# Exchanging the halves of queries and keys: four shifted ScalarE copies, or transfers inside SBUF begun by GpSimd

## The reference, cut to what matters

```python
def apply_rope(t, cos, sin):
    t32 = t.astype(jnp.float32)
    t1, t2 = t32[..., :HEAD_DIM // 2], t32[..., HEAD_DIM // 2:]
    return jnp.concatenate([t1 * cos - t2 * sin, t2 * cos + t1 * sin], axis=-1).astype(t.dtype)

def hybrid_mixer(h, cos, sin, w_in, ...):
    proj = h @ w_in
    q, k, v, x_lru, gate = jnp.split(proj, [...], axis=-1)
    q = apply_rope(q.reshape(bsz, seq, N_Q_HEADS, HEAD_DIM), cos, sin)
    k = apply_rope(k.reshape(bsz, seq, N_KV_HEADS, HEAD_DIM), cos, sin)
    ...
```

## Time and profile before

| | |
|---|---|
| runs, median (range) | 1223.01 us (1222.08 to 1223.96), 3 runs |
| profiled execution, own time | 1217.96 us |
| its span, first to last instruction | 1216.1 us |
| granted TensorE clock, mean | 0.975 of 2.4 GHz |
| PE busy | 1165.7 us, 96% |
| VectorE busy | 864.0 us, 71% |
| ScalarE busy | 545.4 us, 45% |
| GpSimd busy | 13.1 us, 1% |
| HBM traffic | 127 GB/s over the span |

### The profile page before, as it was taken

How to read it: one execution, slowest core, us unless ns; L and a number is a source line. 1 busy time by engine, 2 the same in 40 slices (tenths; PEclk the granted TensorE clock), 3 DMA queues, 4 the chain that set the end, 5 groups by cost and what they waited for, 6 DMA issues and landing times.

```text
span 1216.1 us, 16091 instructions
## 1 busy us (share of the span) xinstructions
PE 1165.7 (96%) x6588; PEld 1010.2 (83%) x6588; DVE 864.0 (71%) x1337; ACT 545.4 (45%) x775; POOL 13.1 (1%) x35
## 2 busy tenths in 40 slices
PE   7989888999899999999999999999999999999995
PEld 7977688988788888888999778988888888888895
DVE  8899988778876777777586997478753656346645
ACT  5579634454324431444346894435531444134430
POOL 4000000000000000000000000000000000000000
PEclk8999988999999999999999999989999999999998
DMA  9632547044684448643222221303333323333212
GB/s 359 232 103 71 190 142 240 1 156 164 219 281 166 150 139 268 222 156 111 83 68 89 69 70 53 105 1 123 103 95 96 104 87 104 91 100 103 88 53 70
DMA packets 44937, 155.78 MB, mean 128 GB/s; under 512 B 5056, under 2 KB 7360, under 8 KB 44864
## 3 DMA queue, kind: packets, MB, share of 16 engines
q1 hardware_dynamic: 44720, 154.23, 38.2%
q10 hardware_dynamic: 144, 0.52, 0.1%
HBM read 152.64 MB, written 2.10 MB: 127 GB/s over the span
## 4 chain that ended last, share of the span: by engine, by line
PE 78%; DVE 12%; DMA 4%; ACT 3%; issue 2%; SPq 1%; DVEq 0%
PE ps L1833 77%; DMA sb_stage<-in_ada 2%; DVE sb_wL L1089 2%; DMA sb_raw<-in_w 2%; DVE sb_R L1559 1%; DVE sb_y L1148 1%; ACT sb_R L778 1%; DVE sb_adaw L1095 1%; DVE sb_x L1152 1%; DVE sb_y L1170 1%; DVE sb_y L1358 1%; ACT sb_hH L605 0%; DVE sb_mL L1380 0%; DVE sb_ssqv L1318 0%; DMA sb_vw<-in_ada 0%
## 5 line engine op out<-in xcount | busy, mean ns | idle before, releaser
L1833 PE MATMUL ps<-sb_hH,sb_wH 128*128 128x512 f32 (+1 forms) x1184 | 424.7, 364 | 7.7 <-ACT sb_hH L605 5.2
L1833 PE MATMUL ps<-sb_hH,sb_wL 128*128 128x512 f32 (+1 forms) x1184 | 418.2, 359 | 0.0
L1833 PE MATMUL ps<-sb_hL,sb_wH 128*128 128x512 f32 (+1 forms) x1184 | 395.1, 358 | 2.7 <-DVE sb_hL L1177 2.7
L1833 PEld LDWEIGHTS ps<-sb_hH,sb_wH 128*128 128x128 f32 x1184 | 228.8, 193 | 43.5 <-ACT sb_hH L605 6.0
L1833 PEld LDWEIGHTS ps<-sb_hH,sb_wL 128*128 128x128 f32 x1184 | 228.7, 193 | 31.7
L1833 PEld LDWEIGHTS ps<-sb_hL,sb_wH 128*128 128x128 f32 x1184 | 214.0, 192 | 35.5 <-DVE sb_hL L1177 3.3
L558 ACT ACTIVATE sb_wH<-sb_raw 128x1024 fp32r<-128x1024 f32 x174 | 181.5, 1050 | 138.3 <-DMA sb_raw<-in_w 138.1
L1089 DVE TENSOR_TENSOR sb_wL<-sb_raw,sb_wH 128x1024 fp32r<-128x1024 f32 x174 | 211.4, 1219 | 38.3 <-ACT sb_wH L558 38.1
L1833 PE MATMUL ps<-sb_mH,sb_wH 128*128 128x256 f32 (+1 forms) x608 | 207.0, 341 | 3.7 <-ACT sb_mH L992 3.5
L1833 PE MATMUL ps<-sb_mL,sb_wH 128*128 128x256 f32 (+1 forms) x608 | 205.9, 339 | 1.7 <-DVE sb_mL L1533 1.7
L1833 PE MATMUL ps<-sb_mH,sb_wL 128*128 128x256 f32 (+1 forms) x608 | 205.3, 338 | 0.0
(11 more groups left out here) (223 smaller groups left out, 1098.3 us busy)
## 6 DMA issues: line engine op xcount, KB each, us to landing
sb_raw<-in_w SPq DMA_DIRECT2D x174, 512.0 KB, 3.7
sb_adaw<-in_ada SPq DMA_DIRECT2D x48, 512.0 KB, 4.4
sb_stage<-in_ada SPq DMA_DIRECT2D x24, 512.0 KB, 11.2
sb_vw<-in_ada SPq DMA_DIRECT2D x24, 512.0 KB, 4.6
sb_side<-in_w SPq DMA_DIRECT2D x8, 512.0 KB, 4.9
sb_raw<-in_w SPq DMA_DIRECT2D x8, 384.0 KB, 14.6
sb_x<-in_x SPq DMA_DIRECT2D x4, 512.0 KB, 5.3
out<-sb_x SPq DMA_DIRECT2D x4, 512.0 KB, 2.9
```

Of the source, the lines that this page charges most:

```text
L1833: return nc.tensor.matmul(out, a, b, start=start, stop=stop, **kw)
```

## The change

ScalarE no longer writes the four shifted blocks. It makes one plain copy of the pair's columns, all 128 partitions, from PSUM to one of two new buffers `rraw`. GpSimd, whose program gets twelve such steps at its end, waits for that copy (`raw_copied`) and begins four transfers, each of 32 partitions by 2 KB (1 KB for narrow pairs), from the copy to the neighbour's block of `swaps`. Each adds 16 to the semaphore of its buffer, so VectorE waits for 64 more on it per turn. The scratch columns of `rsx` move onto columns of `gain1` to make room.

```diff
-        tiny = sb("tiny", [P, 132])
+        tiny = sb("tiny", [P, 128])
...
-        sdx, rsx = tiny[:, 124:128], tiny[:, 128:132]
+        sdx, rsx = tiny[:, 124:128], tiny[:, 96:100]
         edge = sb("edge", [P, GRP, BACK])
+        rraw = [sb("rraw0", [P, SEQ])[:, :], sb("rraw1", [P, SEQ])[:, :]]
...
-        swap_ready, v_pad = sem("swap_ready"), sem("v_pad")
+        raw_copied, swap_ready, v_pad = sem("raw_copied"), [sem("swap_even"), sem("swap_odd")], sem("v_pad")
...
             GTS(nspl[:, :, :], s3, -16.0, 0.0, ALU.mult, ALU.add).then_inc(sp_ready, 1)
+
+            def rope_swaps(l, h, i):
+
+                r = rope_no(l, h, i)
+                cols = slice(0, (2 if i < 2 else 1) * HALF)
+                pool.wait_ge(raw_copied, r)
+                for q4 in range(4):
+                    o = q4 ^ 1
+                    nc.gpsimd.dma_start(swaps[r % 2][32 * q4:32 * q4 + 32, cols],
+                                        rraw[r % 2][32 * o:32 * o + 32, cols]).then_inc(swap_ready[r % 2], 16)
+
+            for l in range(DEPTH):
+                for h in range(2):
+                    for i in range(GRP // 2):
+                        rope_swaps(l, h, i)
...
-                for q4 in range(4):
-                    o = q4 ^ 1
-                    last = nc.scalar.activation(swaps[rope_no(l, h, i) % 2][32 * q4:32 * q4 + 32, cols],
-                                                pair_bank(h, i)[32 * o:32 * o + 32, cols], ACT.Copy)
-                last.then_inc(swap_ready, 1)
+                nc.scalar.activation(rraw[rope_no(l, h, i) % 2][:, cols], pair_bank(h, i)[:, cols],
+                                     ACT.Copy).then_inc(raw_copied, 1)
...
-                dve.wait_ge(swap_ready, r)
+                dve.wait_ge(swap_ready[r % 2], 64 * ((r + 1) // 2))
```

## The result

The changed kernel took 1233.24 us (1232.90 to 1234.33, 4 runs), the kernel before 1222.61 us (1222.08 to 1223.96, 4 runs): ratio 1.0094 (95% interval 1.0082 to 1.0107), so slower by 10.6 us between the medians and 11.5 by the ratio. The profiled execution took 1232.90 us.

A forecast was written before the change was run, and what follows sets the result against it. It took TensorE, busy 96% of the span, as the bound, with ScalarE no bound. Layer 0's 4.9, layer 1's 11.4 and the clock's 0.5 make 16.8, say +17, on 1223: 1240 us, range 1227 to 1260.

The forecast's parts named there:

- The one latency L: Every pair, plain copy's end to last landing: three issues and a landing, 5.8 us taken, bounded by 2.6 and 9.3.
- The signs it named: GpSimd about 4 us per pair; VectorE waiting at first four turns, layer 1 each; TensorE gaps 6.6, 5.6, 5 to 6.
- Its sign of being wrong: GpSimd issues under 0.5 us, which would mean +3 to +7 us for the kernel.
- The term mis-sized first: the issue: GpSimd beginning each transfer, one by one: 1.0 us per issue, GpSimd held 4.0 us per pair.
- held-issues rival: GpSimd issues held by VectorE's work, about 1.6 us each: +37, 1260 us; chance 0.25.
- The term mis-sized second: the landing: Fourth transfer of each pair, from issue to landing: 2.8 us, the row of the 256 KB load.
- Layer 0: Its six turns walked: TensorE's gap before the third turn grows by 3.5; VectorE's lateness reaches TensorE: +4.9 us.
- Layer 1: Its six turns walked: low-halves gap 1.06 becomes 5.6, +10.3 at tile 6, 11.4 at the last x tile's taps.
- Clock: Lower granted clock after layer 1's two TensorE gaps: second's 1.5 us loss covered except about 0.5.
- Nothing later takes it back.: After both layers' turns: the +17 us lasts, since TensorE has almost no gap to the end.
- Cheap transfers: Rival: GpSimd's issue as short as SyncE's, L = 3.0: +3.3, 1226 us; chance 0.20.
- Not slower: Rival at layer 1's first turn: last transfer lands within 1.80 us of the copy, at best 1222 us; chance 0.05.

The follow-up runs named there:

- no_exchange: The kernel before with one plain copy per pair straight into the turn's buffer, the exchange of halves left out (a floor): 1218.33 us, ratio 0.9982.
- before_again: The kernel before, unchanged, run again for a second profile: 1221.59 us, ratio 1.0003.
- copies_unit_later: The kernel before (four copies) with VectorE's dot product of modulation weights moved behind layer 0's third turn: 1217.42 us, ratio 0.9973.
- layer0_only: The changed kernel with transfers in layer 0 alone and the four shifted copies kept in layer 1: 1224.51 us, ratio 1.0021.

## Why the prediction was right, and where its sizes were off

- **Forecast.** 1240 us was given, 1233.2 came, slower as forecast, inside the range and inside the forecast's own 1230 to 1247. The mechanism held in this: ScalarE's relief is worth next to nothing (no_exchange), VectorE waits for the transfers, and through it TensorE. The one latency L for all pairs did not hold, and the agreement is in part luck. With the quiet L of 3.5 us in every pair the prediction's own rule (+3.3 at L = 3.0, about +7 at 4.2) gives some +5, which is an estimate; a collision with weight loads, which no term named, and the clock behind it made up the rest as far as the profiles show.
- **The signs it named.** TensorE's gaps came where it said, at 5.73 us for 6.6 (layer 0's scores), 1.59 and 1.08 for one of 5.6 (the low halves) and 7.12 for 5 to 6 (tile 6). VectorE waited at turns 1 and 4 of layer 0 and at turns 1, 3 and 4 of layer 1, not at the first four of layer 0 and each of layer 1. GpSimd was held 1.97 us per pair, not 4. Its sign of being wrong, issues under 0.5 us with +3 to +7 for the time, came true in its first half (0.498) and not in its second (+10.6), since it took the landing to be the same in every pair.
- **The term mis-sized first: the issue.** 1.0 us was taken, by the longest of SyncE's rows and a GpSimd operation; the trace has 0.50. The SyncE median of 0.33 was the nearer row. On the other side about 0.3 us from the end of the plain copy to the first issue (57.37 to 57.67, 667.17 to 667.46) had no term. The wait for VectorE's work that the held-issues rival assumed does not exist: the shortest issue and the median one took 498 ns, with VectorE busy 3.96 of 4 us beside them (67 to 71 us) and with VectorE busy 0.41 of 4 (668 to 672) alike; the longest of the 48, 726 ns, came in pair 1 of layer 0, with VectorE idle (57 to 61 us). The Trainium skill, page "SBUF — State Buffer", section "SBUF: two separate sides", says that a VectorE operation with two SBUF inputs shuts out only a GpSimd operation that reads SBUF. By that an issue goes through here, and the trace agrees.
- **The term mis-sized second: the landing.** 2.8 us was taken for every pair. It is 1.7 to 2.0 us at the median where few loads are in flight, and up to 8.3 where many are. From the fit in the Trainium skill, page "DMA: Bandwidth & Descriptors", section "Anatomy of one DMA", the estimate for such a piece is 2.15 us. The quiet landings are near it, up to 0.4 shorter, and those beside six weight loads are three times as long. So L, as it turned out, is not one number: from the end of the plain copy to the turn it was 3.5 us at pair 3 of layer 0 (67.66 to 71.14), 3.8 at pair 1 of layer 1 (655.17 to 659.01), 7.5 at pair 1 of layer 0 (57.37 to 64.83) and 10.0 at pair 4 of layer 1 (667.17 to 677.16), where 5.8 was taken for all. The 9.3 at the upper end came from a load's landing of 5.67; it was the right kind of row for pairs 4 and 5 of layer 1, and was exceeded at pair 4.
- **Layer 0**, 2.5 in place of 4.9. The stage is reached 1.35 us later than in the walk (56.77 for 55.42), so the walk's turn 1 would be at 63.25; it was at 64.83, since pair 1 landed beside loads. But pair 3, which TensorE waits for, had the quiet L of 3.5 in place of 5.8. The gap grew by 2.5 (3.23 to 5.73) in place of 3.5, from two errors of opposite sign. VectorE was 3.4 us late at turn 4 (70.88 to 74.31) in place of the walk's 5.2, and 2.5 at the start of layer 1.
- **Layer 1**, 9.1 at tile 6 in place of 10.3. Turn 1 cost 1.9 in place of 4.0, and the low halves 2.67 us of gap (1.59 + 1.08) in place of 5.6. Turn 3 came 3.8 us later (660.88 to 667.19, less layer 0's 2.5), where the walk had 8.6 (landed at 667.5 against 658.9). Then turn 4 waited 8.75 us and gave it back in one step: 10.1 us later (664.57 to 677.16, less 2.5), where the walk had 8.9. The gap ahead of tile 6 is 7.12, not 5.8. What the walk missed is the refills: SyncE begins six loads just as pairs 4 and 5 are under way. The kernel before does the same beside the copies (first load 661.43, fourth exchange from 662.15, in before_again), so this could have been read from its trace.
- **Clock**, 2.8 us behind tile 6's gap (11.6 to 14.5) in place of 0.5: the gap was followed by products at half the clock (0.43 us apart, before 0.23), which was taken to be covered by VectorE's lateness.
- **"Nothing later takes it back."** This step was off by 4.2 us (14.5 to 10.3), more than all terms of the two stages together (14.5 for 16.8). 2.7 of it is the course of the clock behind one later gap, and two profiles of the same kernel drift by 2.8 us over the same stretch. But the medians over four runs each have 10.6 us as well, so it need not be the draw alone; what else took the rest back stays open.
- **Rivals.** Cheap transfers was the nearer one on the quiet prices (L 3.5, where it had 3.0 and the forecast 5.8) and fell at the collision: 1226 was given. Held issues is refuted. Not slower is refuted: no pair landed within 1.80 us of its copy, and no_exchange puts the most that it could have brought at about 2 us.

## What to carry to other kernels

Turning copies on an engine with time to spare into transfers gained nothing here: what counts is the latency up to the consumer, 1.80 us of copies against a start, three issues and a landing, 3.5 us at best. Price a transfer's landing by what else is in flight at that moment, not by the quiet median: look up which loads the same stage releases, and expect a small transfer to land late among them and to make them late in turn. And before moving work off an idle engine, replace it by nothing for one run: no_exchange said in one run that there were 2 us to win, while moving one waiting instruction behind the critical one (copies_unit_later) brought 3.2.

## What the runs showed beside this

**The clock after one and the same gap falls or does not.** At the end of layer 1's mixer TensorE has a gap of about 0.75 us in every profile, in a stretch that the change does not touch. Behind it the granted clock took one of three courses; in before_again it was 0.50 from 752 to 756 us, in the changed kernel 1.00 throughout. In ten us about it, first the second profile of before, then the first profile of before, then the changed kernel:

```profile
748.00:758.00 10.00, 9.25 (x53) 9.17 (x53) 1.12 (x5) 0.27 (x1) 0.00 (x0) 0.66 0.00 1
```

```profile
746.00:756.00 10.00, 9.24 (x65) 9.09 (x65) 2.63 (x8) 1.07 (x3) 0.00 (x0) 0.83 0.00 1
```

```profile
762.00:772.00 10.00, 9.25 (x78) 9.02 (x77) 4.16 (x10) 1.53 (x3) 0.00 (x0) 1.00 0.00 1
```

VectorE's wait for these products tells it in a line, 6.03 us in before_again and 3.31 in the changed kernel:

```profile
757.88 1.40 DVE L1527 SCALAR_TENSOR_TENSOR sb_y<-sb_y,sb_par,ps 128x512 f32<-128x512 f32 x2 [6.03 <-PE ps L1833]
```

```profile
769.27 1.41 DVE L1540 SCALAR_TENSOR_TENSOR sb_y<-sb_y,sb_par,ps 128x512 f32<-128x512 f32 x2 [3.31 <-PE ps L1846]
```

Over the thirteen profiles it was 3.31 three times, 4.82 to 4.85 eight times, 5.90 and 6.03 once each, with and without transfers in each of the first and last kind. It is 2.7 of the 4.2 us by which the lateness shrinks from 14.5 at the x tile to 10.3 at the end; the other 1.5 come in small steps ahead of it and behind it and were not followed up. So part of the difference between two profiles at the end is such a draw. What decides it is not shown.

**The weight loads landed late as well, and for the exchange's sake.** The six 512 KB loads begun from 665.85 to 673.76 landed after 3.6/8.1/10.5 us (min/median/max). In before_again SyncE began six with the same spacing, from 661.4 to 669.3, and in layer0_only from 665.6 to 673.5; layer 1 has copies in both. They landed after 3.6 to 6.8 us there. The lines are for the first four loads, before_again and the change, and for the six of layer0_only (issue view, 665.5 to 676 us: count, KB each, median us to landing):

```profile
DMA to landing us min/median/max: 3.6/5.3/6.8
```

```profile
DMA to landing us min/median/max: 3.6/6.5/10.5
```

```profile
sb_raw<-in_w SPq DMA_DIRECT2D x6, 512.0 KB, 4.6
```

So the delay goes with the exchange's pieces and not with a denser row of loads, though these are only 0.57 MB of the 3.05 moved from 666 to 677 us. The weights' lateness cost nothing of its own as far as VectorE's waits show, since turn 4 was later still (ScalarE had split the two chunks of tiles 6 and 7 by 671.84). Fewer, larger transfers per pair were not tried.
